# When a layer's weight-sum jobs start, and one of them beside the plain down stage

## The reference

```
h = x @ w_in                     # q, k, v of two attentions, and two branch gates
A = differential attention (8 heads; the sample rows also see 512 cached keys and values each)
B = sliding-window attention with sinks (16 q heads, 2 kv heads, window 128)
x = LayerNorm(ALPHA * x + (sigmoid(g_a) * (A @ w_branch_a) + sigmoid(g_b) * (B @ w_branch_b)) @ w_o)
x = LayerNorm(ALPHA * x + relu(x @ w_up) ** 2 @ w_down)
```

## Time and profile before

| | us |
|---|---|
| median of three runs | 2154.99 |
| the profiled execution | 2145.24 |
| its span, first to last instruction | 2143.4 |
| TensorE busy | 2118.8 (99%) |
| VectorE busy | 1471.3 (69%) |
| ScalarE busy | 1230.3 (57%) |
| mean granted TensorE clock | 0.996 of full speed |

### The profile page before, as it was taken

The page is one execution under the profiler, slowest core; times in us unless marked ns, Lnnn a source line. Parts: engine busy times, 40 slices in busy tenths (PEclk is TensorE's granted clock), DMA queues, the critical chain, the costliest instruction groups (busy, mean ns, idle before and its releaser), DMA issues.

```text
span 2143.4 us, 38213 instructions
## 1 busy us (share of the span) xinstructions
PE 2118.8 (99%) x15004; PEld 1936.0 (90%) x15004; DVE 1471.3 (69%) x2336; ACT 1230.3 (57%) x2493; POOL 65.1 (3%) x100
## 2 busy tenths in 40 slices
PE   9999999999989999999999999999999899999998
PEld 7998889999979898989889888899999798989897
DVE  6757777677869356665667577786768693566646
ACT  4457776696525356656234677766865253656561
POOL 1100000001000000000001000000010000000000
PEclk9999999999999999999999999999999999999999
DMA  7877562577894345454368765525778932454541
GB/s 256 240 279 258 210 234 82 159 238 213 222 323 104 103 130 172 151 166 139 108 189 245 289 249 202 205 88 177 223 203 255 294 105 93 139 171 152 168 148 69
DMA packets 100866, 399.27 MB, mean 186 GB/s; under 512 B 15272, under 2 KB 16936, under 8 KB 87600
## 3 DMA queue, kind: packets, MB, share of 16 engines
q1 hardware_dynamic: 67904, 191.55, 26.3%
q0 software_dynamic: 7936, 92.28, 17.2%
q10 hardware_dynamic: 24848, 112.99, 14.7%
HBM read 367.42 MB, written 118.23 MB: 227 GB/s over the span
## 4 chain that ended last, share of the span: by engine, by line
PE 96%; DMA 2%; ACT 1%; DVE 1%; issue 0%; SPq 0%; DVEq 0%; ACTq 0%
PE PS L826 9%; PE PS L828 9%; PE PS L827 9%; PE PS L1047 6%; PE PS L1049 6%; PE PS L1048 6%; PE PS L916 5%; PE PS L917 5%; PE PS L915 5%; PE PS L860 4%; PE PS L861 4%; PE PS L859 4%; PE PS L986 3%; PE PS L987 3%; PE PS L985 3%; PE PS L1175 2%
## 5 line engine op out<-in xcount | busy, mean ns | idle before, releaser
L826 PE MATMUL PS<-xt_hi,w_hi 128*128 128x320 f32 x1184 | 382.1, 323 | 0.3
L828 PE MATMUL PS<-xt_hi,w_lo 128*128 128x320 f32 x1184 | 365.7, 309 | 0.0
L827 PE MATMUL PS<-xt_lo,w_hi 128*128 128x320 f32 x1184 | 365.5, 309 | 0.0
L2539 DVE TENSOR_TENSOR w_lo<-w_raw,w_hi 128x1024 fp32r<-128x1024 f32 x146 | 177.3, 1222 | 162.0 <-ACT w_hi L1577 160.4
L2546 DVE TENSOR_TENSOR w_lo<-w_raw,w_hi 128x1024 fp32r<-128x1024 f32 (+1 forms) x176 | 199.2, 1138 | 114.9 <-ACT w_hi L1593 114.6
L1577 ACT ACTIVATE w_hi<-w_raw 128x1024 fp32r<-128x1024 f32 x146 | 153.3, 1059 | 189.6 <-PE PS L1049 155.8
L826 PEld LDWEIGHTS PS<-xt_hi,w_hi 128*128 128x128 f32 x1184 | 222.7, 188 | 5.4 <-issue 4.3
L827 PEld LDWEIGHTS PS<-xt_lo,w_hi 128*128 128x128 f32 x1184 | 223.0, 188 | 0.1
L828 PEld LDWEIGHTS PS<-xt_hi,w_lo 128*128 128x128 f32 x1184 | 222.2, 188 | 0.0
L1593 ACT ACTIVATE w_hi<-w_raw 128x1024 fp32r<-128x1024 f32 (+1 forms) x176 | 172.2, 984 | 86.1 <-PE PS L987 66.3
L1047 PE MATMUL PS<-w_hi,act_a_hi 128*128 128x512 f32 x480 | 189.7, 395 | 13.2 <-DVE rows L3005 13.2
(11 more groups left out here) (391 smaller groups left out, 5088.2 us busy)
## 6 DMA issues: line engine op xcount, KB each, us to landing
w_raw<-in_weights SPq DMA_DIRECT2D x186, 512.0 KB, 4.6
kc<-in_k_cache ACTq DMA_DIRECT2D x32, 1024.0 KB, 7.5
vc<-in_v_cache ACTq DMA_DIRECT2D x16, 2048.0 KB, 8.7
w_raw<-up_sums SPq DMA_DIRECT2D x112, 256.0 KB, 2.8
up_sums<-in_up_blocks POOLq DMA_DIRECT2D x24, 1024.0 KB, 10.1
w_raw<-in_up_blocks SPq DMA_DIRECT2D x84, 256.0 KB, 2.8
down_sums<-in_down_blocks POOLq DMA_DIRECT2D x16, 1024.0 KB, 10.6
w_raw<-in_down_blocks SPq DMA_DIRECT2D x32, 512.0 KB, 3.5
```

What stands on the lines that cost most here:

```text
L826: mm(out, wh, hi[:, k, c], start=(k == 0), stop=False)
L827: mm(out, wh, lo[:, k, c], start=False, stop=False)
L828: last = mm(out, wl, hi[:, k, c], start=False, stop=(k == KT - 1))
L2539: v.tensor_tensor(w_lo[slot][:], raw[:, raw_of(s, n)[0], :], w_hi[slot][:].bitcast(F32), ALU.subtract)\
```

## The change

Job down 1 waits for the last product with cached values of the layer's eighth head, and no longer for a chunk of the window stage; up 2 and down 2 follow it as before. Job up 3, which had no wait of its own, gets one: for the first chunk of part 0's plain down product. Nothing else is touched.

```diff
@@ -804,7 +804,9 @@
                 if (kind, part) == ("up", 0):
                     pool.wait_ge(w_ready[0], nth(l, AT_V) + 1)
                 elif (kind, part) == ("down", 1):
-                    pool.wait_ge(w_ready[0], nth(l, AT_SWA, 2) + 1)
+                    pool.wait_ge(dec_pv, 2 * HEADS * (l + 1))
+                elif (kind, part) == ("up", 3):
+                    pool.wait_ge(w_ready[0], down_at(l, 0) + 1)
                 (up_sums_of if kind == "up" else down_sums_of)(l, part, JOB_TRANSFERS * j)
```

## The result

| | before | after |
|---|---|---|
| median of 20 runs each, same chip | 2150.46 | 2155.26 |
| lowest to highest | 2142.79 to 2157.53 | 2148.11 to 2163.69 |
| the profiled execution | 2145.24 | 2153.98 |
| its span | 2143.4 | 2152.2 |
| mean granted TensorE clock | 0.996 | 0.994 |

The ratio after to before is 1.003, with a 95% interval of 1.0016 to 1.0043. The forecast had been 2148, the profiled execution 7 us shorter. It became 8.7 us longer.

The account below looks back on a forecast made before the run. TensorE's waits and low clock at the first LayerNorm, 17.5 us, were the loss to win. -17 there, +10 in branch A, 0 at the down stage: -7, 2138 profiled, 2148 median; own range 2141 to 2153, 8 in 10: 2134 to 2159.

Parts of the forecast that it names:

- What bounds the kernel: First LayerNorm of both layers: TensorE's waits of 13.2 us plus 4.3 us of low clock, 17.5 us, beside job up 3.
- The wait at the LayerNorm goes: First LayerNorm: weight loads land in time once no job runs there; 17 us gained, bounds none to 17.5.
- Rival B: First LayerNorm stays starved, loads late by 3 or 4 us: 9 won, 10 given back, 2156; chance 0.15.
- Up 3 at the down stage costs 0: Plain down stage: job up 3 beside it costs TensorE 0, at most 7 us a layer.
- rival D: Down stage: up 3 costs what it cost before, 7 us in each layer, giving 2162; chance 0.03.
- What the jobs now lie beside: Branch A, 348 to 425 us: late gate loads cost 5 us a layer, 10 in all; bounds 0 to 12 a layer.
- the main load of branch A: Gate load issued at 403.63, right behind up 2's two adds: 1.9 to 4.4 us over its limit, say 3.2.
- the limit of 8 us: Branch A: the gate load issued at 403.63 may take 3.85 + 4.1 = 8 us before TensorE waits.
- the prediction's second value of 4.4: Branch A: the gate load issued at 403.63 waits for the adds' end near 416, 4.4 us over its limit.
- the load at 391.3: Branch A gate load just ahead of up 2's two puts: 0 to 2.5 us late, taken as 1.25.
- those that were given 0 to 1 us together: Branch A's other late gate loads, beside single transfers that are over in time: 0 to 1 us together, taken as 0.5.
- Rival C: Branch A's two gate buffers become the limit: 24 us lost against 17 won, 2162; chance 0.1.

Follow-up runs that it names:

- jobs 16 us later: Kernel after, without branch A's gate loads from the third tile on, jobs begun at the last head's normalisation, some 16 us later: 2141.73, ratio 0.9965.
- the order exchanged: Kernel after, with the window attention's cached values issued ahead of its cached keys, both by ScalarE: 2151.16, ratio 0.9996.

## Why the prediction was wrong, step by step

*What bounds the kernel* was right: the 17.5 us lay at the LayerNorm, up 3 caused them, and moving up 3 alone is worth 0.9%. That run's profile shows 2133.53 against 2145.24, 11.7 us, of which the waits give 9.8. The ratio of 0.9911 stands for 19 us. The clock accounts for most of the rest: its mean over the runs is 0.9988 here and 0.9948 in before, and 0.0040 of 2119 us busy is 8.5 us.

*The wait at the LayerNorm goes*: right, and more fully than 17 of 17.5. Rival B, which had it starved still, is refuted: the weight load issued between 610 and 620 lands in 4.3 us. With up 3 moved alone, 3.4 us of it stay.

*Up 3 at the down stage costs 0*: right, and with it rival D falls.

*What the jobs now lie beside*: this is the step that failed. Its working for the main load of branch A held: the limit of 8 us, the load that would break it, the wait there (3.2 forecast; 3.8 and 3.3 measured). That load landed 3.3 us before the two adds were over, so it did not wait for their end, as the prediction's second value of 4.4 had it. (The limit took half high parts at 0.5 us; they last 0.63, which lowers it by 0.3 at most.) That the sum agrees as well (10 forecast, 10.2 measured) is in part luck: the load at 391.3, which was to cost 1.25 us, cost nothing, and the other two waits came from a load beside a single add, one of those that were given 0 to 1 us together. The step failed because it was sized for one stage and one kind of load. I followed the jobs up to 425 and stopped, though by my own times they went on to 510.6, through the window attention. There I never asked what ScalarE issues, and took an issue for something that costs its few tenths of a microsecond, as L2244 does. Two terms are missing from the sum: the hold on ScalarE behind the cached keys, 8.6 us, and TensorE's low clock behind the new waits, 8.8 us. I had priced that clock at the LayerNorm as part of the gain (4.3 us behind two waits) and forgot to price it behind the waits that I forecast. With both, the sum is -17.5 + 10.2 + 8.6 + 8.8 = +10. The median hides part of the miss: the profiled execution was to be 7 us shorter and is 8.7 longer. The 9.75 us set on it for the median came from three runs; over twenty that distance is 5.2 us in before, and 1.3 in after.

The Trainium skill, DMA: Bandwidth & Descriptors, section on specifications, gives 512 bytes as the least size of a transfer at full rate. The keys' pieces have 256. The trace shows that small pieces alone aren't slow enough to make the hold: as the add ended, the keys went through within 3 us (433 to 436). It is beside large transfers that they stand. That larger pieces would not be held was not tried.

*Rival C* had the sign and nearly the size, a loss of 7, by the wrong price: it had 24 us in branch A alone, where 10.2 were measured.

*How long the hold lasts.* Issues of `s_v` by ScalarE took 1.3 to 1.6 us with no job. With one they took 4.8 to 8.9 beside adds; beside puts mostly 2.5 to 4.0, but 6.6 and 4.8 with all jobs a head earlier. What sorts them is not the kind of the step but the time that it has left. Seven kernels have a job running there, in two layers each; in all fourteen cases the last held issue (that of `s_v`, or of `mix_a` behind it) ended within 1.2 us of the start of the job's next step. The 6.6 us are such a case: the issue at 436.78 ended at 443.35, and the puts beside it at 444.23. The adds only last longer, two of them 15 us and more. What stays open is what in the queue stops the issue, and what shorter steps would bring: no run changed the length of a step and nothing else.

The best kernels found are before with up 3's wait alone (0.9911) and the one with down 1 in the heads besides (0.9923). Their intervals overlap, and they weren't run on one chip together, so the smaller edit is the one to take.

## What to carry to other kernels

When background transfers are moved, list every load that each engine issues in the new place, with the time it has, and among them the issues themselves: behind a load of many small pieces the next issue can hold the engine for as long as the pieces take to drain, which in these runs was until the large transfer beside them was over. Charge each forecast wait of TensorE with the clock behind it too; here it added 8.8 us to 18.8 us of waits. And try the parts of a change alone: one of these parts was worth 0.9%, and the other took it back.

## What the hardware showed that was not expected

- An issue of a 256 KB load held ScalarE 1.38 us with no job beside it, 8.03 and 8.88 us beside accumulating copies in device memory, 6.57 us beside plain ones, and SyncE up to 14.52 us. It depends on what stands ahead in that queue: with the order exchanged the same issue took 0.53 us.
- Beside two accumulating copies, ScalarE's queue and GpSimd's moved 60 packets each in 3 us (1490 to 1493, jobs 16 us later), packets of 256 bytes in the one and of 8 KB in the other: 0.02 MB against 0.49.
- TensorE's granted clock was at 0.50 from 440 to 444, after 2.7 us of idle time between 436 and 440, and at 0.81 in the 4 us after that.
- Two accumulating copies of 1 MB each took 17.1 us from their issue to the next step beside branch A (401.71 to 418.80), and 23.2 us beside the last head's cache loads (317.94 to 341.18).
